# A hybrid attention and state-space block: most on-chip turns of activations moved from TensorE transposes to DMA transposes of 16-bit planes

## What is computed

```python
hn = rms_norm(h, mix_norm_w)
proj = hn @ w_in                         # 2048 x 20544, one projection
q, k, v, z, xbc, dt_raw, gate_logits = split(proj)
q, k = per-head rms_norm of q and k      # 16 heads of 128
attn = moba_attention(q, k, v)           # 256 tokens: one causal block, ALiBi
y_attn = attn @ w_attn_out
y = grouped_rms_norm(ssd_scan(conv(xbc), dt) * silu(z)) * norm_w   # 256 x 4096
y_ssm = y @ w_ssm_out                    # 4096 x 2048
h = h + (g_attn * y_attn + g_ssm * y_ssm) @ w_out
u = rms_norm(h, mlp_norm_w) @ w_up       # 2048 x 8192
h = h + square(relu(u)) @ w_down         # 8192 x 2048
```

## Time and profile before

| | before |
|---|---|
| median of 3 executions | 2037.79 us (2037.73 to 2037.82) |
| the profiled execution's own time | 2037.69 us |
| its span, first to last instruction | 2035.5 us |
| TensorE busy | 2030.2 us, 100% |
| VectorE, ScalarE, GpSimd busy | 1232.8, 1060.1, 195.1 us |
| share of 16 DMA engines | 64.9% on the main queue |

### The profile page before, as it was taken

One profiled execution on the slowest core, in us unless ns is written; L12 is line 12 of the kernel. 1 busy time (PEld: TensorE's weight loads), 2 busy tenths in 40 slices (PEclk: granted clock), 3 DMA queues, 4 the chain that ended last, 5 costly groups with the idle time before them and its releaser, 6 DMA issues.

```text
span 2035.5 us, 26734 instructions
## 1 busy us (share of the span) xinstructions
PE 2030.2 (100%) x9286; PEld 1686.7 (83%) x9286; DVE 1232.8 (61%) x1372; ACT 1060.1 (52%) x1249; POOL 195.1 (10%) x206
## 2 busy tenths in 40 slices
PE   9999999999999999999999999999999999999999
PEld 8888888888888888888888888888888888888887
DVE  5666565776677666666655555556545655654654
ACT  6454555766666554545564444455435534544542
POOL 2110010011131111111210000000000000000000
PEclk9999999999999999999999999999999999999999
DMA  7656556787766666665555666667667767766775
GB/s 243 188 166 176 167 171 178 207 219 216 206 197 194 190 197 199 198 193 183 176 174 189 194 188 226 196 196 214 202 195 216 209 195 204 205 209 195 202 223 163
DMA packets 254447, 399.87 MB, mean 196 GB/s; under 512 B 69008, under 2 KB 69968, under 8 KB 254112
## 3 DMA queue, kind: packets, MB, share of 16 engines
q1 hardware_dynamic: 252944, 395.31, 64.9%
q10 hardware_dynamic: 960, 2.75, 0.4%
q0 software_dynamic: 464, 0.77, 0.2%
HBM read 382.46 MB, written 2.16 MB: 189 GB/s over the span
## 4 chain that ended last, share of the span: by engine, by line
PE 99%; DMA 0%; ACT 0%; DVE 0%; SPq 0%; issue 0%; DVEq 0%
PE ps L502 31%; PE ps L504 31%; PE ps L503 31%; PE ps L471 2%; PE ps L717 1%; PE ps L556 0%; PE ps L579 0%; PE ps L706 0%; DMA raw<-in_w_in 0%; PE ps L727 0%; PE ps L580 0%; PE ps L557 0%; PE ps L612 0%; PE ps L614 0%; DVE wlo L1292 0%; ACT whi L855 0%
## 5 line engine op out<-in xcount | busy, mean ns | idle before, releaser
L1292 DVE TENSOR_TENSOR wlo<-raw,whi 128x1024 fp32r<-128x1024 f32 x703 | 889.4, 1273 | 650.9 <-ACT whi L855 648.4
L855 ACT ACTIVATE whi<-raw 128x1024 fp32r<-128x1024 f32 x703 | 738.9, 1058 | 680.1 <-PE ps L504 657.4
L502 PE MATMUL ps<-whi,xT_hi 128*128 128x512 f32 x1276 | 508.7, 399 | 0.2 <-DVE wlo L1292 0.2
L504 PE MATMUL ps<-whi,xT_lo 128*128 128x512 f32 x1276 | 498.2, 390 | 0.0
L503 PE MATMUL ps<-wlo,xT_hi 128*128 128x512 f32 x1276 | 497.2, 390 | 0.0
L504 PEld LDWEIGHTS ps<-whi,xT_lo 128*128 128x128 f32 x1276 | 239.5, 188 | 50.9
L503 PEld LDWEIGHTS ps<-wlo,xT_hi 128*128 128x128 f32 x1276 | 240.1, 188 | 48.2 <-issue 1.0
L502 PEld LDWEIGHTS ps<-whi,xT_hi 128*128 128x128 f32 x1276 | 239.9, 188 | 48.3 <-issue 1.5
L502 PE MATMUL ps<-whi,fT_hi 128*128 128x512 f32 x512 | 199.4, 389 | 0.2 <-DVE fT_lo L1729 0.2
L502 PE MATMUL ps<-whi,hT_hi 128*128 128x512 f32 x512 | 199.4, 389 | 0.0
L504 PE MATMUL ps<-whi,hT_lo 128*128 128x512 f32 x512 | 199.3, 389 | 0.0
(11 more groups left out here) (258 smaller groups left out, 1884.1 us busy)
## 6 DMA issues: line engine op xcount, KB each, us to landing
raw<-in_w_in SPq DMA_DIRECT2D x319, 512.0 KB, 3.9
raw<-in_w_up SPq DMA_DIRECT2D x128, 512.0 KB, 4.3
raw<-in_w_down SPq DMA_DIRECT2D x128, 512.0 KB, 4.4
raw<-in_w_ssm_out SPq DMA_DIRECT2D x64, 512.0 KB, 4.3
raw<-in_w_attn_out SPq DMA_DIRECT2D x32, 512.0 KB, 4.3
raw<-in_w_out SPq DMA_DIRECT2D x32, 512.0 KB, 4.4
arow<-arows SPq DMA_DIRECT2D x16, 512.0 KB, 4.9
h<-in_x ACTq DMA_DIRECT2D x1, 2048.0 KB, 11.0
```

The costliest lines, as they stand in the source:

```text
L502: mm(dst, xh, whi[sl][:, kk, :], start=(s == 0 and kk == 0), stop=False)
L504: last = mm(dst, xl, whi[sl][:, kk, :], start=False, stop=(s == US - 1 and kk == UK - 1))
L855: A(whi[s % SLOTS][:, :, :], raw[s % SLOTS][:, :, :], ACT.Copy).then_inc(hi_ready, 1)
L1292: V.tensor_tensor(wlo[s % SLOTS][:, :, :], raw[s % SLOTS][:, :, :], fp(whi[s % SLOTS][:, :, :]), ALU.subtract).then_inc(lo_ready, 1)
```

## The change

The q, y and most of the merged and h tiles go the second way. For q (4 groups), y (8 groups of the scan), column blocks 0 to 2 of the merged branches, and column blocks 0 and 1 of h, the eight TensorE transposes go away; a halving copy on ScalarE, two DMA transposes on SyncE and two joining copies on VectorE take their place. The hi and lo parts are then taken from SBUF. k, the last merged block and h's blocks 2 and 3 stay on TensorE. GpSimd's copies of y (`y_copy`) go away. The halving of a tile, its turns, its join and the hi and lo parts are put at different steps, over one to two blocks. Three loops of the lists for SyncE, ScalarE and VectorE are written out. What is left out below is the same pattern with other names.

```diff
+        q_half = sb("q_half", "E", 0, [P, 2, NTOK, COLS], u16)
+        q_tiles = sb("q_tiles", "E", 4 * KB, [P, 2, NTOK * 4, P], u16)
+        q_turn_st = sb("q_turn_st", "E", 8 * KB, [P, 4, T])
...
+        y_half = [sb(f"y_half{i}", "W", 4 * KB * i, [P, 2, NTOK, GW], u16) for i in range(2)]
+        y_tiles = [sb(f"y_tiles{i}", "W", 8 * KB + 4 * KB * i, [P, 2, NTOK * 4, P], u16) for i in range(2)]
+        yT = sb("yT", "W", 16 * KB, [P, 4, T])
...
+        m_half = sb("m_half", "W", 4 * KB, [P, 2, NTOK, COLS], u16)
+        m_tiles = sb("m_tiles", "W", 12 * KB, [P, 2, NTOK * 4, P], u16)
+        mT = sb("mT", "W", 16 * KB, [P, 4, T])
+        h_half = sb("h_half", "W", 0, [P, 2, NTOK, COLS], u16)
...
+            def q_turn(g, a):
+                sp.wait_ge(q_halved, g + 1)
+                if g:
+                    sp.wait_ge(q_joined, g)
+                sp.dma_start_transpose(q_tiles[:, a, :, :], q_half[:, a, :, :].rearrange("p t n -> p (t n)")) \
+                    .then_inc(q_turned, 16)
+
...
+            def h_turn(j, a):
+                sp.wait_ge(h_halved, j + 1)
+                if j:
+                    sp.wait_ge(h_joined, j)
+                else:
+                    sp.wait_ge(m_joined, 3)
+                sp.dma_start_transpose(m_tiles[:, a, :, :], h_half[:, a, :, :].rearrange("p t n -> p (t n)")) \
+                    .then_inc(h_turned, 16)
...
+            def y_turn(G, a):
+                sp.wait_ge(y_halved, G + 1)
+                if G > 1:
+                    sp.wait_ge(y_joined, G - 1)
+                else:
+                    sp.wait_ge(ysq_done, 16)
+                sp.dma_start_transpose(y_tiles[G % 2][:, a, :, :], y_half[G % 2][:, a, :, :].rearrange("p t n -> p (t n)")) \
+                    .then_inc(y_turned[G % 2], 16)
+
+            def gate_turns(jb, s):
+
+                if jb and s in (0, 1):
+                    y_turn(2 * jb - 2, s)
+                if jb and s in (4, 5):
+                    y_turn(2 * jb - 1, s - 4)
+
...
+                    if m is not None and s in (2, 3):
+                        m_turn(m, s - 2)
+                    if h is not None and s in (2, 3):
+                        h_turn(h, s - 2)
+                    if q is not None and s >= US - 2:
+                        q_turn(q, s - US + 2)
+                    if gate is not None:
+                        gate_turns(gate, s)
...
+            load_block(B_QKV + 2, w_in, 0, V0, q=0)
...
+                load_block(B_QKV + 3 * g + 2, w_in, 0, V0 + g * COLS, q=g)
...
+            for j in range(4):
+                load_block(B_GATE + j, w_in, 0, GATE0 + D + j * COLS, gate=j)
+            load_block(B_SSM, w_ssm_out, 0, 0, gate=4)
+            load_block(B_SSM + 1, w_ssm_out, D, 0)
+            for j in range(1, 4):
                 load_block(B_SSM + 2 * j, w_ssm_out, 0, j * COLS)
-                load_block(B_SSM + 2 * j + 1, w_ssm_out, D, j * COLS)
-            with sp.Fori(0, 4) as j:
-                load_block(B_OUT + j, w_out, 0, j * COLS)
...
+                put(0, lambda: pe.wait_ge(kT_ready, g + 1))
+                put(0, lambda: pe.wait_ge(qT_ready, g + 1))
...
+            def k_transposes(g):
+                def f():
+                    pe.wait_ge(qk_normed, 2 * g + 2)
+                    pe.wait_ge(set_free[1], g + 1)
+                    for hh in range(4):
+                        for t in range(NTOK):
+                            o = (hh % 2) * T + t * P
+                            last = transpose(SETS[1][hh // 2][:, o:o + P], k_st[:, t, hh * HD:(hh + 1) * HD])
...
-            def y_transposes(G, i):
-                def f():
-                    pe.wait_ge(y_copied, G + 1)
-                    for c in range(4):
-                        for t in range(NTOK):
-                            o = (c % 2) * T + t * P
-                            last = transpose(ps[4 + 2 * i + c // 2][:, o:o + P], y_st[i][:, t, c * P:(c + 1) * P])
-                    last.then_inc(y_T, 1)
-                return f
-
             with pe.Fori(0, 2) as i:
                 for k in range(2):
-                    jb = 2 * i + k
-                    G = 2 * jb
-                    stream(B_GATE + jb, k, 18 + i, xT_hi, xT_lo,
-                           after={2: [y_transposes(G, 0)], 6: [y_transposes(G + 1, 1)]})
-
-
...
-                stream(B_OUT + j, j % 2, 24 + j // 2, gT_hi, gT_lo, after={2: [h_transposes(j - 1)]})
+                stream(B_OUT + j, j % 2, 24 + j // 2, gT_hi, gT_lo, after={2: [h_transposes(2)]} if j == 3 else None)
...
+            def q_halve(g):
+                def f():
+                    act.wait_ge(qk_normed, 2 * g + 1)
+                    if later(g):
+                        act.wait_ge(q_turned, 32 * g)
+                    A(q_half[:, :, :, :].rearrange("p a t n -> p a (t n)"),
+                      halves(q_st[:, :, :].rearrange("p t n -> p (t n)")), ACT.Copy).then_inc(q_halved, 1)
+                return f
+
+            def copy_qT(g):
+                def f():
+                    act.wait_ge(q_joined, g + 1)
+                    act.wait_ge(const_ready, 2)
+                    if later(g):
+                        act.wait_ge(scores, 4 * g)
+                    A(qT[:, :, :], q_turn_st[:, :, :], ACT.Copy, scale=par[:, QN_C:QN_C + 1]).then_inc(qT_ready, 1)
+                return f
...
+            steps(B_QKV + 1, {1: [dtT_copy], 2: [dt_chain], 6: [q_halve(0)], 7: [evac_qk(0, 1, k_st)]})
+            steps(B_QKV + 2, {1: [dec_chain], 4: [evac_kT(0)], 5: [copy_qT(0)], 7: [evac_v(0)]})
...
+                add(a[1], 5, q_halve(g))
...
+                add(a[2], 5, copy_qT(g))
...
+            def y_halve(G):
+                def f():
+                    act.wait_ge(yfin, 2 * G + 2)
+                    if G > 1:
+                        act.wait_ge(y_turned[G % 2], 32 * (G // 2))
+                    else:
+                        act.wait_ge(y_mm, 16)
+                        act.wait_ge(yz_done, 8)
+                    A(y_half[G % 2][:, :, :, :].rearrange("p a t n -> p a (t n)"),
+                      halves(xs[:, G, :, :].rearrange("p t n -> p (t n)")), ACT.Copy).then_inc(y_halved, 1)
+                return f
...
+                steps(B_GATE + jb, {0: [y_halve(2 * jb)], 2: [s_hi(2 * jb - 1)] if jb else [],
+                                    4: [y_halve(2 * jb + 1)], 6: [s_hi(2 * jb)],
+                                    7: [sgate_evac(B_GATE + jb, jb % 2, jb)]})
...
+            def m_halve(j):
+                def f():
+                    act.wait_ge(m_ready, j + 1)
...
+            steps(B_SSM, {2: [s_hi(7)], 7: [half_evac(0)]})
             steps(B_SSM + 1)
             with act.Fori(1, 4) as j:
-                steps(B_SSM + 2 * j, {3: [g_hi(j - 1)], 7: [half_evac(j)]})
-                steps(B_SSM + 2 * j + 1)
+                steps(B_SSM + 2 * j, {2: [m_halve(j - 1)], 7: [half_evac(j)]})
...
+            def h_halve(j):
+                def f():
+                    act.wait_ge(set_free[j], 25)
+                    if j:
+                        act.wait_ge(h_turned, 32 * j)
+                    else:
+                        act.wait_ge(set_free[1], 24)
+                    A(h_half[:, :, :, :].rearrange("p a t n -> p a t n"),
+                      h[:, :, j * COLS:(j + 1) * COLS].bitcast(u16).rearrange("p t (n a) -> p a t n", a=2),
+                      ACT.Copy).then_inc(h_halved, 1)
...
+            steps(B_OUT + 1, {1: [h_squares(0)], 2: [h_halve(0)]})
+            steps(B_OUT + 2, {1: [h_squares(1)], 2: [h_halve(1)], 4: [h_hi_joined(0)]})
+            steps(B_OUT + 3, {1: [h_squares(2)], 2: [h_hi(2)], 4: [h_hi_joined(1)]})
...
+                add(a[2], 4, q_join(g))
...
+            def y_join(G):
+                def f():
+                    dve.wait_ge(y_turned[G % 2], 32 * (G // 2) + 32)
+                    if G:
+                        dve.wait_ge(sT_lo_done, 4 * G)
+                    for a in range(2):
+                        i = V.tensor_copy(halves(yT[:, :, :].rearrange("p c t -> p (c t)"))[:, a, :],
+                                          y_tiles[G % 2][:, a, :, :].rearrange("p (t c) l -> p c t l", t=NTOK))
+                    i.then_inc(y_joined, 1)
+                return f
...
+                steps(B_GATE + jb, {1: [y_join(2 * jb - 1)] if jb else [], 3: [s_lo(2 * jb - 1)] if jb else [],
+                                    5: [y_join(2 * jb)], 7: [s_lo(2 * jb)]})
...
+            steps(B_SSM, {1: [y_join(7)], 3: [s_lo(7)]})
             steps(B_SSM + 1, {7: [merge_ssm(0)]})
             with dve.Fori(1, 4) as j:
-                steps(B_SSM + 2 * j, {3: [g_lo(j - 1)]})
-                steps(B_SSM + 2 * j + 1, {7: [merge_ssm(j)]})
-
+                steps(B_SSM + 2 * j)
...
+            steps(B_OUT + 1, {7: [h_add(1)]})
+            steps(B_OUT + 2, {2: [h_join(0)], 5: [h_lo_joined(0)], 7: [h_add(2)]})
+            steps(B_OUT + 3, {2: [h_join(1), h_lo(2)], 5: [h_lo_joined(1)], 7: [h_add(3)]})
```

(67 more changed lines are left out.)

202 lines of the change are left out of this document (108 added, 94 removed).

## The result

The changed kernel takes 2023.43 us (median of four executions, 2023.27 to 2024.20) against 2037.76 us, a ratio of 0.9929 with a 95% interval of 0.9916 to 0.9941: 14.3 us or 0.7% faster. The profiled execution took 2023.30 us, with a span of 2021.6.

What follows compares the result with a forecast made beforehand. TensorE was taken as the bound: 2037.69 us less 15.3 for 136 removed transposes plus 0.2 at the first k block gave 2022.6, stated as 2022.5 us; range 2021.3 to 2026.5 us, chance 0.81.

Steps and rivals of the forecast that it cites:

- TensorE is the bound and removed time comes back in full: Whole kernel: TensorE busy 2030.2 of 2035.5 us, so taking 136 transposes off it saves 15.3 us.
- The price: 0.109 us in a row, 0.91 for a lone group of eight: Transposes on TensorE, priced by chain distances: four q groups at 0.87 us, 13 others at 0.91, sum 15.3 us.
- The rival of the 272 ns record: Each transpose costs TensorE its 272 ns record: 136 make 37.0 us, time 2000.7 us; chance 0.02.
- The work added is hidden: Halvings, DMA issues and joins for 17 tiles cost 0; second gate ScalarE and VectorE each 66 of some 87 us.
- The waits for raw weights: ScalarE waiting for weight loads queued on SyncE: a few us in all.
- The first k block: First q halving waits for normalised q and delays k's evacuation and norm: 0 to 0.9 us, taken as 0.2.
- DMA load: Second gate: a tile's pair of DMA transposes costs 3.8 us of all 16 engines; two pairs fit in a 21.76 us block.
- The rival built on it: DMA transposes shut out second gate weight loads: 9.2 us a pair, 29 us lost, 2051 us; chance 0.03.
- Ten microseconds of lead behind SyncE: SyncE's weight loads: 4.2 us spare before ScalarE waits, 5.8 more before TensorE does, 10 in all.
- The figures of the Trainium skill: DMA pair estimated at 1.4 us; TensorE transpose about 275 ns, giving 37 us; its rule would make no such change.
- Costing the edits of the lists themselves at nothing: Engine instruction lists: writing the loops out was costed at nothing, as none of these engines is the bound.

Runs made afterwards that it cites:

- the groups of sixteen: Changed kernel with sixteen spare transposes on TensorE at each of eight places in the second gate, 128 in all: 2035.85 us.
- spare transposes: Changed kernel with all 136 removed transposes back on TensorE at their old places, turning the identity into unread banks, DMA way kept: 2037.66 us.
- the doubled turns: Changed kernel with each of the 16 DMA transposes of y issued twice, the second into an unread tile: 2025.66 us, repeated 2025.32 us.

## Why the prediction was right, point by point

- *TensorE is the bound and removed time comes back in full.* Right: 15.3 us by the MLP's start, and putting the 136 back took all of that away.
- *The price: 0.109 us in a row, 0.91 for a lone group of eight.* Right to 0.1 us in the sum (4 x 0.87 + 13 x 0.91); the groups of sixteen came to 1.79 each. The rival of the 272 ns record would have needed 2000.7 us and is out.
- *The work added is hidden.* Right: with spare transposes beside the DMA way the distance to the MLP is that of the kernel before, and leaving out y's transposes gives nothing. In the second gate ScalarE is busy 65 us for a forecast of 66, VectorE 59, also for a forecast of 66; the blocks are 21.76 us apart, as forecast. The waits for raw weights, forecast at a few us in all, are 22.5, but they were 22.3 before.
- *The first k block.* The evacuation of k was forecast at about 62.3 us and came at 62.18; the norm of k was to end between 72.3 and 75.1 and ended at 71.61 + 1.23 = 72.8. Due was 74.3, so the cost was 0 where I took 0.2. VectorE's timeline of the changed kernel, which answers to the earlier trace rows:

```profile
71.61 1.23 DVE L1514 TENSOR_TENSOR k_st<-k_st,rqk 128x1024 f32<-128x1024 f32 x1 [0.25 <-POOL rqk L2005]
```

- *DMA load.* The forecast share of the second gate was 0.95, measured 0.91, so 3.4 us a pair for 3.8. The use I made of it was wrong: share 1 is no limit, as the doubled turns showed. The rival built on it (2051 us at 9.2 us a pair, slower from 8 us) has its condition unmet, and as share 1 is no limit, its threshold doesn't follow. The margin was larger than stated.
- *Ten microseconds of lead behind SyncE.* Right for ScalarE's wait (4.76 us forecast as 4 to 5), wrong as a bound for TensorE: a late turn also holds VectorE at its join. It didn't matter for the forecast, as no turn of the change waits long.
- *The figures of the Trainium skill.* By the Trainium skill (Advanced Engine Details and Errata, X-Bar Transpose) a pair was estimated at 1.4 us; this case's share gives 3.4, and 1.9 for each pair added on top. The rule of the Trainium skill (VectorE: DVE Perf Modes, Rules for kernel authors) would have kept the transposes on TensorE; here TensorE was the bound, and moving them gave 14.3 us.
- *The step that was missing.* Costing the edits of the lists themselves at nothing. With TensorE's shorter list the MLP loop's instructions are loaded on every pass, and the jumps bring 1.5 us of stalls; less the 0.3 of a late lo part in the kernel before, 1.1 net. With the loop written out the kernel takes 2022.00. Two terms went the other way: the k block cost nothing (0.2 forecast), and 0.4 us fell away around the span, which wasn't forecast. Without these the time would have been some 2024, so part of the nearness of 2022.5 to 2023.43 is luck. The mechanism and its price are not: they show in the distance to the MLP, 15.30 us for a forecast of 15.3.

## What to carry to other kernels

Where TensorE is busy all the time, price what is taken off it by the distances in the chain, not by the records, and check the result at a landmark in the middle of the run, so that a loss elsewhere isn't booked on the change. In this kernel, moving work to DMA was free while each DMA's input was ready when its turn in the issuing queue came and each consumer stood well behind its landing; one tile's turns a block placed too early cost 8 us. So count for every wait what is queued behind it on both the issuing and the consuming engine. After a change of the list's length, look at the loop jumps for time named issue and at the packets of the instruction queue, and try the loop written out.

## What the runs showed of the hardware

- TensorE stalled 0.25 to 1.5 us above the usual distance at the jumps of a loop of 768 matmuls, each with its weight load, in five of the nine forms that have this loop (four of the five have the same list for TensorE). They load 66 packets of 16 KB of instructions in an execution; the four forms that don't stall load 48, none of them in the loop's second and third pass.
- Sixteen float32 transposes of 128x128 take TensorE 1.75 us in a row, though the record of one is 272 ns; 136 of them in groups cost 15.3 us.
- The DMA share of a stretch went to 1.12 with 268 GB/s and 1.09 with 288 GB/s, without a wait of TensorE in these blocks.
- TensorE stood 4.2 us between two matmuls; 1.3 us after it resumed the granted clock fell to 1.2 GHz, for some 3.4 us, which cost 1.6 us more.
